# Second attention of a hybrid encoder step: the reciprocal sum applied by a diagonal in the transposing product instead of by a GpSimd pass

## The chip, the cores and the metric

The kernel runs on one core of one Trainium2 chip. The metric is the device time of one execution in microseconds (us); lower is better. A core has five engines with a queue of their own each: TensorE (PE, matrix products; PEld is its weight load), VectorE (DVE), ScalarE (ACT), GpSimd (POOL) and SyncE (SP, which issues the DMAs). They run side by side and wait for each other with semaphores.

## The reference, cut to what matters

Two transformer layers run over 512 prompt tokens and 32 sample tokens. Each layer has two groups of eight attention heads, and the change touches the second group only:

```python
logits = einsum('bqhd,bqkhd->bqhk', qb, ks) * dh ** -0.5
logits = logits + bias
logits = where(valid, logits, -inf)
p = softmax(logits, axis=-1)
return einsum('bqhk,bqkhd->bqhd', p, vs)
```

The kernel does not gather keys. It computes the logits of all keys and adds a large negative number where a key was not among the top-k of its query (the tile `excl`).

## The kernel before, in words

All activations are kept transposed (features on the 128 partitions, 544 tokens along the free dimension). Everything that an engine does is one list of steps (`schedule()`), written out once and walked by each engine's block; an engine does only those steps that concern it, in the order of the list. Two layers are two turns of one loop over this list.

Large products (`G` steps, `L1103` to `L1107`) are made of three products of split operands: `w_hi` is written by ScalarE (`L836`), `w_lo` by GpSimd (`L1623`), from the weights that SP has loaded to `raw`.

The second attention is `b_phase()`. Its unit is a tile: one head and one block of 128 queries, against the keys up to the end of that block, so that tiles are 128, 256, 384 and 512 wide (`b_width`), in chunks of 128 keys. There are 8 heads with 4 blocks each, and two sample tiles of width 288: 34 tiles and 86 chunks in a layer. A tile goes through these steps:

- `BL`: TensorE makes the logits in PSUM (`L1276`, `L1277`). VectorE adds the bias and takes the row maximum (`L1587`) and negates it (`L1589`).
- `BX`: ScalarE takes the exponential into `prob[:, i % 2]` and sums each row into `stat` (`L961`).
- In the `BL` step of the next tile VectorE takes the reciprocal of that sum (`L1593`), and GpSimd multiplies `prob` with it, row by row (`L1638`).
- `BT`, two tiles later: TensorE transposes the chunks of `prob` (`L1286`), and ScalarE copies them to `wts` (`L976`, `L978`, for the sample tiles `L969`, `L970`).
- `BV`, once for each head: TensorE multiplies with the values (`v_product`, `L624`), and VectorE copies the result to `o_t` (`L689`).

The order on TensorE in iteration `i` is `BL(i)`, then `extra[i]`, `BV`, `BT(i - 2)`, and then `late[i]`. The lists `extra` and `late` hold the other work of the phase: the `G` products of the next pair of heads, the sums of their norms (`N`, `L1142`, which wait for ScalarE's squares `L859`), VectorE's norm steps (`E` is `L1475`, `N` is `L1382`, `M` is `L1399` to `L1406`, `W` is `L1417` to `L1430`), the transposes `T` (`L1155`), and on VectorE rounds of top-k of the sample (`TOPK`, `L663`, `L666`). These `G` products end with the fourth pair of heads; the last heads (steps from about 413 us in the first layer) have none beside them until the output projection begins.

## Time and profile before

| | |
|---|---|
| median of 3 runs | 1780.64 us (1780.3 to 1781.72) |
| the profiled execution, its own time | 1778.47 us |
| its span in the trace | 1776.6 us |
| PE busy | 1658.8 us (93%) |
| PEld busy | 1516.1 us (85%) |
| DVE busy | 1014.6 us (57%) |
| ACT busy | 686.6 us (39%) |
| POOL busy | 648.4 us (36%) |
| mean granted TensorE clock | 0.981 of full speed |

Busy shares are averages over stages with different limits. The second attention lies at about 315 to 445 us of the span in the first layer and 1180 to 1306 us in the second. In a row, `xN` is a count; times in brackets are idle time of the engine just before, with what ended it. A plain float32 product stands in the trace with two records of each kind (two PEld, two PE) for each product, a transposing one with one of each.

### The profile page before, as it was taken

Reading aid. Unit: us, or ns where it says so; the run is one execution under the profiler, and the core shown is the slowest. Engines: PE = TensorE matmul, PEld = TensorE weight load, DVE = VectorE, ACT = ScalarE, POOL = GpSimd, SP = SyncE. Lnnn points to the kernel's source line nnn. Section 1 sums busy time; section 2 is a strip of 40 time slices with the busy share of each in tenths; the row PEclk is TensorE's granted clock in tenths of the full one; section 3 lists DMA queues with packets and bytes.
Section 4 is the critical chain, followed back from the end, with each engine's and each line's share of the span. In section 5 each row is a group of like instructions: output and inputs, shape, how many; then the busy total and the mean of one; then the engine's idle time right before and its main releaser. Section 6 shows DMA issues by size and latency. Waiting matters only on the chain.

```text
span 1776.6 us, 33458 instructions
## 1 busy us (share of the span) xinstructions
PE 1658.8 (93%) x11748; PEld 1516.1 (85%) x11762; DVE 1014.6 (57%) x1865; ACT 686.6 (39%) x1282; POOL 648.4 (36%) x352
## 2 busy tenths in 40 slices
PE   6898999887999999999989999989789999999998
PEld 4677888775999999999986878867579999999998
DVE  5466666574566526616656666667636662563366
ACT  3232444344344324424433144534533442342343
POOL 3222332232544334344441232323336434433334
PEclk9899999899899999999999999999989999999999
DMA  5223121210222322322232222121102233233222
GB/s 166 78 64 91 49 55 48 62 43 19 60 84 84 93 86 85 95 84 84 77 88 73 86 68 68 36 76 35 37 25 84 84 93 87 84 90 89 84 82 91
DMA packets 238231, 131.78 MB, mean 74 GB/s; under 512 B 10126, under 2 KB 232062, under 8 KB 238054
## 3 DMA queue, kind: packets, MB, share of 16 engines
q1 hardware_dynamic: 238054, 129.52, 25.5%
q8 instruction: 98, 1.61, 0.4%
q14 instruction: 79, 0.65, 0.1%
HBM read 117.59 MB, written 11.62 MB: 73 GB/s over the span
## 4 chain that ended last, share of the span: by engine, by line
issue 38%; PE 26%; POOL 23%; DVE 7%; ACT 3%; DVEq 1%; ACTq 1%; POOLq 0%; DMA 0%; SPq 0%; another core or an unknown queue 0%
POOL w_lo L1623 20%; PE g_ps L1103 5%; PE g_ps L1104 5%; PE g_ps L1107 5%; PE a_ps L624 2%; POOL h_lo L578 2%; PE a_ps L1181 1%; PE a_ps L1276 1%; PE g_ps L1142 1%; DVE score L1532 1%; POOL sp_lo L1632 1%; PE a_ps L1193 1%; DVE score L666 1%; PE a_ps L1286 1%; ACTq L920 1%
## 5 line engine op out<-in xcount | busy, mean ns | idle before, releaser
L1623 POOL TENSOR_TENSOR w_lo<-raw,w_hi 128x1024 fp32r<-128x1024 f32 (+2 forms) x210 | 503.1, 2396 | 803.2 <-ACT w_hi L836 803.2
L1103 PE MATMUL g_ps<-h_hi,w_hi 128*128 128x272 f32 (+1 forms) x1632 | 452.8, 295 | 17.6 <-DVEq L1492 8.1
L1104 PE MATMUL g_ps<-h_lo,w_hi 128*128 128x272 f32 (+1 forms) x1632 | 444.0, 290 | 0.0
L836 ACT ACTIVATE w_hi<-raw 128x1024 fp32r<-128x1024 f32 (+2 forms) x210 | 217.4, 1035 | 499.1 <-PE g_ps L1107 377.9
L1107 PE MATMUL g_ps<-h_hi,w_lo 128*128 128x272 f32 (+1 forms) x1632 | 340.8, 290 | 0.0
L1103 PEld LDWEIGHTS g_ps<-h_hi,w_hi 128*128 128x128 f32 (+1 forms) x1632 | 309.1, 189 | 29.6 <-issue 18.0
L1104 PEld LDWEIGHTS g_ps<-h_lo,w_hi 128*128 128x128 f32 (+1 forms) x1632 | 308.8, 189 | 0.5
L1107 PEld LDWEIGHTS g_ps<-h_hi,w_lo 128*128 128x128 f32 (+1 forms) x1632 | 257.3, 189 | 0.0
L1501 DVE SCALAR_TENSOR_TENSOR wts<-work,par,wts 128x546 f32<-128x546 f32 x176 | 196.8, 1118 | 100.0 <-ACT wts L1002 92.1
L1103 PE MATMUL a_ps<-h_hi,w_hi 128*128 128x272 f32 x704 | 190.3, 288 | 1.5 <-POOL w_lo L1623 1.5
L1104 PE MATMUL a_ps<-h_lo,w_hi 128*128 128x272 f32 x704 | 190.0, 289 | 0.0
L1107 PE MATMUL a_ps<-h_hi,w_lo 128*128 128x272 f32 x704 | 145.9, 288 | 0.0
L1103 PEld LDWEIGHTS a_ps<-h_hi,w_hi 128*128 128x128 f32 x704 | 132.5, 188 | 1.9 <-POOL w_lo L1623 1.9
L1104 PEld LDWEIGHTS a_ps<-h_lo,w_hi 128*128 128x128 f32 x704 | 132.5, 188 | 0.0
L1107 PEld LDWEIGHTS a_ps<-h_hi,w_lo 128*128 128x128 f32 x704 | 110.1, 188 | 0.0
L1103 PE MATMUL g_ps<-act_hi,w_hi 128*128 128x272 f32 x376 | 102.6, 291 | 4.7 <-DVEq L1514 3.6
L1002 ACT ACTIVATE wts<-work,par 128x546 f32<-128x546 f32 x88 | 74.4, 846 | 75.6 <-DVEq L581 75.5
L1104 PE MATMUL g_ps<-act_lo,w_hi 128*128 128x272 f32 x376 | 101.5, 289 | 0.0
L1638 POOL TENSOR_SCALAR prob<-prob,stat 128x128 f32<-128x128 f32 (+2 forms) x68 | 48.1, 708 | 143.8 <-DVE stat L1593 143.7
L1103 PE MATMUL a_ps<-act_hi,w_hi 128*128 128x272 f32 x328 | 88.8, 289 | 1.2 <-POOL w_lo L1623 1.2
L1478 DVE TENSOR_TENSOR x_t<-x_t,g_ps 128x544 f32<-128x544 f32 x42 | 30.3, 721 | 103.9 <-PE g_ps L1107 102.6
L1104 PE MATMUL a_ps<-act_lo,w_hi 128*128 128x272 f32 x328 | 88.5, 288 | 0.0
(223 smaller groups left out, 2994.1 us busy)
## 6 DMA issues: line engine op xcount, KB each, us to landing
raw<-in_w_up SPq DMA_DIRECT2D x88, 512.0 KB, 3.8
raw<-in_w_in SPq DMA_DIRECT2D x56, 512.0 KB, 3.8
raw<-in_w_down SPq DMA_DIRECT2D x32, 512.0 KB, 3.9
raw<-in_w_out SPq DMA_DIRECT2D x16, 512.0 KB, 3.9
raw<-in_w_down SPq DMA_DIRECT2D x16, 384.0 KB, 3.4
x_nat<-in_x_prompt SPq DMA_DIRECT2D x4, 512.0 KB, 6.4
strip<-bias_line SPq DMA_DIRECT2D x8, 256.0 KB
out_p_av<-v_nat SPq DMA_DIRECT2D x4, 512.0 KB, 3.8
```

The lines of the kernel that those rows point to most:

```text
L578: pool.tensor_tensor(h_lo[:, j, :], prob_f(j), h_hi[:, j, :].bitcast(F32), ALU.subtract).then_inc(x_split.sem, 1)
L624: mm = pe.matmul(a_ps[3][:, c * P:SEQ], v_nat[:, c, p * P:(p + 1) * P], w_view(wts, c), start=(c == 0), stop=(c == QB - 1), skip_group_che ...
L666: dve.match_replace(s, top8[0:n, i, :], s, TAKEN)
L836: act.activation(w_hi[:, n % SPLIT, 0:kt, 0:c], raw[:, n % RAW, 0:kt, 0:c], ACT.Copy).then_inc(hi_done.sem, 1)
L1002: act.activation(cbuf[kind], ubuf[kind][:, 2:U], ACT.Identity, bias=par[:, 3, col:col + 1], scale=par[:, 2, col:col + 1]).then_inc(c_tap.s ...
L1103: pe.matmul(g[0:c, a, 0:HALF], w_hi[:, s, j, 0:c], xh[:, mov], start=(j == 0), stop=False)
L1104: pe.matmul(g[0:c, a, 0:HALF], w_hi[:, s, j, 0:c], xl[:, mov], start=False, stop=False)
L1107: mm = pe.matmul(g[0:c, a, 0:HALF], w_lo[:, s, j, 0:c], xh[:, mov], start=False, stop=(j == kt - 1))
L1478: dve.tensor_tensor(halves(x_t[:, m, :]), halves(x_t[:, m, :]), g, ALU.add)
L1501: dve.scalar_tensor_tensor(c, u[:, tap:tap + U - 2], par[:, tap, col:col + 1], c, ALU.mult, ALU.add)
L1623: pool.tensor_tensor(w_lo[:, s, 0:kt, 0:c], raw[:, n % RAW, 0:kt, 0:c], w_hi[:, s, 0:kt, 0:c].bitcast(F32), ALU.subtract).then_inc(lo_done ...
L1638: pool.tensor_scalar(prob[:, i % 2, 0:w], prob[:, i % 2, 0:w], stat[:, i % 4, 3:4], 1.0, ALU.mult, ALU.mult).then_inc(b_nrm.sem, 1)
```

## The change

GpSimd no longer takes part in the second attention. VectorE, after the reciprocal, waits for its own result (`drain`) and multiplies the 128x128 identity, row by row, with the reciprocal sums; this writes a diagonal matrix into one of two buffers `diag`, which lie over the first 256 columns of `work`. TensorE multiplies each chunk of raw exponentials, as the stationary operand, with that diagonal; the result in PSUM is the transposed and normalised chunk. It waits for `b_diag` where it waited for `b_nrm`. VectorE's wait for `b_nrm` of four tiles before is gone (a semaphore increment stands there).

```diff
+        diag = work[:, 0:2 * P].rearrange("p (a c) -> p a c", a=2)
...
-        b_rcp = ev("b_rcp", btiles)
-        b_nrm = ev("b_nrm", btiles)
+        b_diag = ev("b_diag", btiles)
...
                     elif k == "BT":
                         i = st[1]
-                        pe.wait_ge(b_nrm.sem, b_nrm.at(l, btiles[i]))
+                        pe.wait_ge(b_diag.sem, b_diag.at(l, btiles[i]))
...
                         for c in range((w + P - 1) // P):
                             n = min(P, w - c * P)
-                            mm = pe.transpose(a_ps[2][0:n, c * P:(c + 1) * P], prob[:, i % 2, c * P:c * P + n], ident)
+                            mm = pe.matmul(a_ps[2][0:n, c * P:(c + 1) * P], prob[:, i % 2, c * P:c * P + n], diag[:, i % 2, :], start=True, stop=True)
...
                             dve.wait_ge(bl_full.sem, bl_full.at(l, t))
-
-                            if i >= 4:
-                                dve.wait_ge(b_nrm.sem, b_nrm.at(l, btiles[i - 4]))
-                                dve.sem_inc(spacer, 1)
-                            else:
-                                dve.wait_ge(b_nrm.sem, b_nrm.last(l, btiles[i - 4]))
-                                dve.sem_inc(spacer, 1)
+                            dve.sem_inc(spacer, 1)
+
...
                         if i:
                             dve.wait_ge(b_exp.sem, b_exp.at(l, btiles[i - 1]))
                             s = (i - 1) % 4
-                            dve.reciprocal(stat[:, s, 3:4], stat[:, s, 2:3]).then_inc(b_rcp.sem, 1)
+                            dve.reciprocal(stat[:, s, 3:4], stat[:, s, 2:3])
+                            dve.drain()
+                            dve.tensor_scalar(diag[:, (i - 1) % 2, :], ident, stat[:, s, 3:4], None, ALU.mult).then_inc(b_diag.sem, 1)
...
-                    elif k == "BL" and st[1]:
-                        i = st[1] - 1
-                        w = b_width(btiles[i])
-                        pool.wait_ge(b_rcp.sem, b_rcp.at(l, btiles[i]))
-                        pool.sem_inc(spacer, 1)
-                        pool.tensor_scalar(prob[:, i % 2, 0:w], prob[:, i % 2, 0:w], stat[:, i % 4, 3:4], 1.0, ALU.mult, ALU.mult).then_inc(b_nrm.sem, 1)
```

The order of instructions on SP and ACT is the same in both kernels. On TensorE the place of each instruction stays; what the `BT` steps read changes. This is TensorE's order around the third and fourth tile of a head, of the difference between the two kernels (`cf` holds the identity, `work` the diagonals):

```order
-L1286 MATMUL a_ps<-cf,prob 128x128 x2
+L1286 MATMUL a_ps<-work,prob 128x128 x2
 L1261 REGISTER_ALU
 L1276 MATMUL a_ps<-k_t,q_pad 128x128
 L1277 MATMUL a_ps<-excl,cb 128x128
-L1286 MATMUL a_ps<-cf,prob 128x128 x3
+L1286 MATMUL a_ps<-work,prob 128x128 x3
```

Nothing moved there; each `L1286` product has become a plain one.

On VectorE each tile gets one more instruction. This is the order of the kernel before in the first head, from the maximum of the 512 wide tile to the norm's `W` step (`q_pad`):

```order
L1587 ISA a_ps,stat<-a_ps,strip 128x512
L1587 ISA stat 128x1
L1589 TENSOR_SCALAR stat<-stat 128x1
L1593 RECIPROCAL stat<-stat 128x1
L1417 SCALAR_TENSOR_TENSOR q_pad<-nraw,qk_gain,vb 64x544 x2
```

And this is the same place in the changed kernel (its lines are counted anew):

```order
L1582 ISA a_ps,stat<-a_ps,strip 128x512
L1582 ISA stat 128x1
L1584 TENSOR_SCALAR stat<-stat 128x1
L1588 RECIPROCAL stat<-stat 128x1
L1590 TENSOR_SCALAR work<-cf,stat 128x128
L1417 SCALAR_TENSOR_TENSOR q_pad<-nraw,qk_gain,vb 64x544 x2
```

The diagonal is built behind the reciprocal and ahead of whatever VectorE does next, here the norm's writing of `q_pad`.

## Rows read from the trace of the kernel before

**Rows 1.** Busy time of each engine in both second attentions, with clock
```profile
core 0: us, PE busy (x) PEld busy (x) DVE busy (x) ACT busy (x) POOL busy (x), PEclk, DMA share, GB/s
315.00:445.00 130.00, 108.85 (x623) 83.83 (x628) 77.66 (x228) 55.62 (x150) 38.10 (x40) 0.96 0.15 43
1180.00:1306.00 126.00, 105.03 (x593) 80.29 (x599) 76.70 (x223) 54.89 (x148) 38.12 (x40) 0.96 0.15 44
```

**Rows 2.** Waits of TensorE over the span: who for whom, total, times, longest
```profile
PE a_ps L1286 <- POOL prob L1638: 10.8, 11, 2.0
PE g_ps L1103 <- POOL w_lo L1623: 6.8, 7, 2.3
```

**Rows 3.** Groups by form: busy us, mean ns, then idle time before
```profile
L1286 PE MATMUL a_ps<-cf,prob 128*128 128x128 f32 x168 | 32.4, 293 | 21.4 <-POOL prob L1638 10.8 <-ACT wts L976 9.1 <-ACT wts L970 1.4
L1276 PE MATMUL a_ps<-k_t,q_pad 128*128 128x128 f32 x32 | 6.4, 284 | 0.0
```

**Rows 4.** Timeline of TensorE, first attention: start us, us, engine, line
```profile
290.63 0.38 PE L1201 MATMUL a_ps<-work,cr 128*128 128x128 f32 x2
290.85 0.39 PE L1209 MATMUL a_ps<-work,cr 128*128 128x128 f32 x2
```

**Rows 5.** VectorE's and GpSimd's groups by form
```profile
L1593 DVE RECIPROCAL stat<-stat 128x1 f32<-128x1 f32 x68 | 10.5, 154 | 8.7 <-ACT prob L961 8.2 <-issue 0.5
L1530 DVE TENSOR_SCALAR score<-prob,iw_nat 128x512 f32<-128x512 f32 x2 | 1.0, 487 | 2.3 <-ACT prob L913 2.3
L1530 DVE TENSOR_SCALAR score<-prob,iw_nat 128x256 f32<-128x256 f32 x2 | 0.7, 352 | 3.9 <-ACT prob L913 3.9
L1638 POOL TENSOR_SCALAR prob<-prob,stat 128x256 f32<-128x256 f32 x16 | 12.5, 778 | 49.3 <-DVE stat L1593 49.3
...
L1638 POOL TENSOR_SCALAR prob<-prob,stat 128x128 f32<-128x128 f32 x16 | 9.4, 589 | 16.5 <-DVE stat L1593 16.4
```

**Rows 6.** Timeline, first head of the first layer, all engines
```profile
327.79 0.84 DVE L1401 TENSOR_TENSOR va<-va,vb 128x544 f32<-128x544 f32 x1
328.71 0.72 DVE L1406 SCALAR_TENSOR_TENSOR vb<-va,vb 128x544 f32<-128x544 f32 x1
336.74 0.66 ACT L859 ACTIVATE sq<-nraw 128x544 f32<-128x544 f32 x1 [2.95 <-DVEq L581]
337.54 2.15 PE L1142 MATMUL g_ps<-sq,cf 128*128 128x272 f32 x4 [3.75 <-ACT sq L859]
340.55 1.06 PE L1286 MATMUL a_ps<-cf,prob 128*128 128x128 f32 x4
341.40 1.23 PE L1276 MATMUL a_ps<-k_t,q_pad 128*128 128x384 f32 x2
```

**Rows 7.** Timeline, second pair of heads, all engines
```profile
353.44 1.06 ACT L836 ACTIVATE w_hi<-raw 128x1024 fp32r<-128x1024 f32 x1 [1.51 <-PE g_ps L1107]
355.02 0.63 PE L1286 MATMUL a_ps<-cf,prob 128*128 128x128 f32 x4 [0.75 <-ACT wts L976]
355.92 1.16 PE L1142 MATMUL g_ps<-sq,cf 128*128 128x272 f32 x4 [0.27 <-ACT sq L859]
371.90 0.66 PE L1286 MATMUL a_ps<-cf,prob 128*128 128x128 f32 x4 [0.23 <-POOL prob L1638]
374.01 2.42 PE L624 MATMUL a_ps<-wts,v_nat 128*128 128x512 f32 x8 [0.65 <-ACT wts L978]
```

**Rows 8.** Timeline, third pair and a head without filler, all engines
```profile
409.95 0.63 PE L1155 MATMUL g_ps<-cf,k_t 128*128 128x128 f32 x4 [1.23 <-DVEq L1431]
421.63 0.15 DVE L1593 RECIPROCAL stat<-stat 128x1 f32<-128x1 f32 x1
421.99 1.22 POOL L1638 TENSOR_SCALAR prob<-prob,stat 128x512 f32<-128x512 f32 x1 [0.32 <-DVE stat L1593]
423.26 0.65 PE L1286 MATMUL a_ps<-cf,prob 128*128 128x128 f32 x4 [0.44 <-POOL prob L1638]
```

**Rows 9.** Timeline of TensorE, end of the first layer's phase; last row second layer
```profile
434.91 0.60 PE L1286 MATMUL a_ps<-cf,prob 128*128 128x128 f32 x4
440.52 0.49 PE L1286 MATMUL a_ps<-cf,prob 128*128 128x128 f32 x3
441.72 0.52 PE L1286 MATMUL a_ps<-cf,prob 128*128 128x128 f32 x3 [0.71 <-ACT wts L970]
1275.17 1.06 PE L1286 MATMUL a_ps<-cf,prob 128*128 128x128 f32 x4
```

More of the change, by code:

```diff
@@ L1344, in _ @@
             dve.drain()
-            for s in g_free + [v_done, r_done, e_done, kc_done, i_add, tk_done, a_min, a_sp, s_lo0, o_out, b_max, b_rcp, o_split, sqx_done, c_done, a_prod, a_lo]:
+            for s in g_free + [v_done, r_done, e_done, kc_done, i_add, tk_done, a_min, a_sp, s_lo0, o_out, b_max, b_diag, o_split, sqx_done, c_done, a_prod, a_lo]:
                 dve.sem_inc(s.sem, s.per_layer)
@@ L1608, in _ @@
         def _(pool):
-            for s in (lo_done, s_lo, b_nrm):
+            for s in (lo_done, s_lo):
                 pool.sem_inc(s.sem, s.per_layer)
```

## The prediction, made before the changed kernel ran

> **What bounds the kernel now.** I read the page's busy shares first: TensorE 93%, nothing else above 57% except its own weight load. The change touches only the second attention, so next I read the windows of its two stretches [rows 1]: TensorE is busy 108.9 of 130 us and 105.0 of 126, VectorE 77.7 and 76.7, GpSimd 38 and 38. So TensorE has some 21 us without a matrix product in each stretch, a sixth, and whatever is added to it is paid in full wherever it is not falling into one of these gaps. Third, the waits: over the span TensorE waits 10.8 us in 11 waits for GpSimd's normalised `prob` [rows 2]. That is what the change can remove. Its waits for `w_lo`, the other work of GpSimd, are 6.8 us over the whole span in front of the `g_ps` products [rows 2], and the timeline shows hardly any of them in these stretches, so a freer GpSimd is worth about nothing by itself. Last I walked the timeline of one layer's phase and asked at each `BT` what the next wait of TensorE would be.
>
> **Part 1: the transposing products become plain ones.** There are 86 chunks in a layer, 172 in all. Each is one record now (168 with 128 columns and 4 with 32) [rows 3]. The nearest plain product of the same size, `L1276` with 128 columns, has two records for each product (32 for 16 tiles) of the same length, 284 ns against 293. How far apart they start is told by the first attention: `L1201` and `L1209` are two such products with different weights, and the second starts 0.22 us after the first [rows 4], so 0.11 us a record. So a chunk costs 0.11 us more at the high clock level (2.4 GHz). At the low one (1.2 GHz) four chunks took 0.85 us (340.55 to 341.40, [rows 6]), 0.21 a record, so 0.21 more each. All 172 in the open would be 172 x 0.11 = 18.9 us; none, 0. I take neither end but count the places below.
>
> In these 172 records the weight load could set the pace instead. The products of rows 4 show that it does not at 128 columns, over four records; over eight I have no row, and allow up to 0.15 us a record for the upper end (that is 172 x 0.04 x 2 = 14 us more at worst, all in the open, which I think unlikely).
>
> The Trainium skill ("TensorE: Matmul & The Clock Gate", Terms) says that the transpose mode is 4 times faster for float32, and "Perfetto Trace Analysis" (Transposes) tells one to use it and no plain product. The trace agrees on the direction, not on the size: its rows give a factor of 2 in records and the same length for each. By the factor of 4 each chunk would cost 0.33 us more, and the sum would be up to 57 us. It has 1 chance in 100.
>
> **Part 2: GpSimd's pass becomes VectorE's diagonal.** GpSimd took 0.59 to 0.78 us a tile, and in one place 1.22 us, plus some 0.2 us from the reciprocal's end to its start (421.63 + 0.15 to 421.99) [rows 5, 8]. VectorE now takes the drain, about 0.08 us as between other dependent pairs, and a 128 wide multiply by a column. No row has that width; `L1530` with 512 and 256 takes 487 and 352 ns [rows 5], which is 0.53 ns a column, so 128 would be 0.285 us. Its bounds are the one-column reciprocal, 0.154 us, and the 256 wide one, 0.352. I take 0.285 and with the drain 0.36 us a tile. So the diagonal is ready 0.36 us after the reciprocal, where `prob` was ready after 0.8 to 1.4: 0.5 to 1.0 us sooner. VectorE gets 68 x 0.36 = 24.5 us more, 12 a layer, beside 77.7 of 130: it stays below TensorE, but 0.36 us is paid where VectorE is the one that TensorE waits for.
>
> **The sum, by places, for one layer.**
> - First head. TensorE idles 3.75 us before the `N` products, for a chain of VectorE's norm steps that ends in ScalarE's square (which itself idled 2.95 us for VectorE) [rows 6]. Two diagonals fall in that chain: +0.72. The six chunks before it are hidden by the wait. The four behind it run at the low level: +0.85. One more chunk ahead of `G` products: +0.11. Together 1.7.
> - Second pair of heads (20 chunks). Three chunks lie in front of `G` products and delay them: 0.33. The three at 353 us are hidden: ScalarE's `w_hi`, 1.06 us, holds up what comes next [rows 7]. The four at 355.02 end 0.27 us before the `N` products [rows 7]: 0.44 more is 0.15 in the open. Five at 367 to 369 us are hidden by the wait for the next square. The four at 371.90 start sooner, as they waited for GpSimd, and have until 374.01, where TensorE waits for ScalarE anyway: hidden, but a diagonal ahead of VectorE's `L1382` pushes the norm chain by 0.13. One chunk more at 376: 0.11. Together 0.7.
> - Third pair. The same 0.7, and here TensorE waits 1.23 us for VectorE's `k_t` [rows 8], with a diagonal in the chain: +0.36, and two chunks right behind: +0.22. Together 1.3.
> - The two heads without filler. Here the chain of work runs reciprocal, GpSimd, `BT` [rows 8]. At 421.63 the new diagonal is ready, with the one before it pushing VectorE by 0.36, about 0.5 us sooner than `prob` was; four chunks with 0.44 more eat that up. Net 0 to 0.15 a head, and a chunk behind `BV` 0.11: together 0.4.
> - The end: the wait at 430 us is 0.1 shorter on balance, and then the chunks at 434.91, 440.52 and 441.72 [rows 9] have output products or other waits behind them that move with them: 0.44 + 0.33 + 0.33. Together 1.0.
>
> That is 5.1 us a layer. In the second layer four chunks at 1275.17 are at the low level [rows 9] and so are some at 1285: 0.7 more. 5.1 + 5.8 = 10.9. Against it stands one gain: VectorE's two-input `L1401` takes 0.84 us beside GpSimd's pass and `L1406` 0.72 without it [rows 6]; some 8 such places on the path at 0.1 us give back 0.8. The Trainium skill ("GPSIMD Engine Reference", Key points) says that the two engines share their SBUF interfaces and contend when VectorE reads two inputs from there; by that rule the gain is real, and the trace agrees, with 0.12 us at this place; without the rule the sum would be 10.9.
>
> So +10.1 us. The profiled execution took 1778.47 us (its span 1776.6 and 1.9 around it), which gives 1788.6. The median of the runs is 2.2 above that execution, so the forecast for the median is **1790.7 us**, 0.6% slower.
>
> **The rivals.**
> - *The latency wins* (faster). The 11 waits for GpSimd shrink by 0.5 to 1.0 us each, and the extra records hide, because a `BT` that started sooner still ends before ScalarE wants it. For it: in the heads without filler the chain of work runs through GpSimd. Against it: the point from which it decides is a saving above 0.55 us for a tile of four chunks (5 x 0.11), and only the one 1.22 us pass is clearly above. Its time: 11 x 0.5 = 5.5 less, 1775.1.
> - *The gaps swallow it* (no change). TensorE's 42 us without work are larger than 18.9, and if the extra records fell into them everywhere, the saved waits would pay for the rest: 1780.6, give or take 3. Against it: most gaps are before `N` and `T` steps, and two chunks in five do not stand there.
> - *Everything in the open* (slower still). TensorE pays 18.9 + 1.5 for the low level, and VectorE's diagonals some 2: 1780.6 + 22.4 = 1803. For it: TensorE's share of 84%. Against it: the waits of 0.75 and 3.75 us right beside `BT` steps.
> - *The clock.* TensorE's clock fell to the low level after its 3.75 us of idling. If the changed kernel idles less ahead of the second layer's last heads and keeps the high level there, about 2 us come back; if it falls elsewhere, as much is added. It goes into the range.
> - *The change does not do what it says:* if the plain products had one record each, only part 2 were left, about -3 us: 1777.6. `L1276` speaks against it; it counts with the first rival.
>
> **How the numbers follow.** Forecast 0.70; everything in the open (with the factor of 4) 0.10; no change 0.11; faster 0.09. What a measurement can tell from no change is about 0.2%, 3.6 us; the forecast's own spread (1785 to 1797) is above that. So slower 0.80, same 0.11, faster 0.09. The range goes from 1780, which leaves out the faster rival and some of no change, to 1800.
>
> **What would show it.** In the changed kernel's profile: `L1286` with 336 + 8 records and a gap of 0.11 us between them; the new `TENSOR_SCALAR` with 68 at 0.22 to 0.35 us; no wait of TensorE for `prob`, and new ones for VectorE's diagonal of at most a few us; the stretch of the phase 5 to 6 us longer in each layer, and nothing changed outside. The prediction is wrong if the stretches are not longer, if records start more than 0.13 us apart, or if the diagonal takes over 0.4 us.

## The result, and the profile after

The changed kernel took 1793.78 us (median of 4 runs, 1792.9 to 1796.8), the kernel before 1780.47 us beside it (4 runs, 1774.87 to 1781.72): a ratio of 1.0084, 95% interval 1.0059 to 1.0108 (the ratios here compare all runs of both; the two medians alone give 1.0075). It is slower, by about 13 us where 10 were forecast. Beside the experiments the changed kernel ran again: 1793.55 us against 1776.45, and the ratio was 1.0101 (1.0083 to 1.0118).

The profiled execution took 1793.21 us, its span 1791.3. The two phases of the second attention (from the first logits product `L1276` to the end of the last `L1300`, the sample's product with the values) and the two gated networks behind them, in the changed kernel (start and end, length, busy time and records of TensorE, its weight load, VectorE, ScalarE and GpSimd, granted clock, DMA share, GB/s):

```profile
314.38:450.25 135.87, 120.77 (x716) 96.18 (x722) 88.45 (x260) 55.94 (x150) 14.17 (x6) 0.96 0.14 41
1184.64:1320.49 135.85, 120.74 (x716) 96.19 (x722) 88.44 (x260) 55.93 (x150) 14.16 (x6) 0.96 0.14 41
504.70:886.00 381.30, 373.76 (x2946) 370.96 (x2945) 201.53 (x314) 141.94 (x245) 150.48 (x64) 1.00 0.29 84
1375.00:1755.90 380.90, 373.34 (x2947) 370.53 (x2946) 201.38 (x314) 141.96 (x245) 150.54 (x64) 1.00 0.29 84
```

And the kernel before, between the same marks. The windows of [rows 1] end at other places of the work, so the phases are given again; the rows ahead of the prediction do not show the networks, as nobody looked there:

```profile
315.75:448.34 132.59, 111.44 (x630) 85.94 (x636) 77.22 (x226) 55.62 (x150) 38.10 (x40) 0.95 0.14 42
1178.07:1310.58 132.51, 111.54 (x631) 86.03 (x636) 77.34 (x227) 55.64 (x150) 38.12 (x40) 0.95 0.14 42
503.00:879.70 376.70, 372.41 (x2946) 370.72 (x2945) 194.17 (x314) 142.11 (x245) 151.22 (x64) 1.00 0.30 85
1365.90:1742.60 376.70, 372.43 (x2947) 370.72 (x2946) 194.24 (x314) 142.10 (x245) 151.22 (x64) 1.00 0.30 85
```

In each phase TensorE has 9.3 and 9.2 us more work, VectorE 11.2 and 11.1 more, GpSimd 24 less, and each phase is 3.3 us longer, not the 5 to 6 that the prediction gave as its sign. But the networks, in whose code not one line changed and whose record counts are the same to within one, are some 4 to 5 us longer each. VectorE's busy time is what differs most in them: 7.4 and 7.1 us more for the same 314 records.

Read stage by stage, in us. The attention stage goes from the first logits product to the first norm product (`L1136`) behind the output projection, the network from there to the first product that transposes its tails (`L1161`), which stands close to its end:

| stage | before | after | difference |
|---|---|---|---|
| up to the first attention product of layer 1 | 315.75 | 314.38 | -1.4 |
| attention and output projection, layer 1 | 187.30 | 190.30 | +3.0 |
| network, layer 1 | 376.67 | 381.37 | +4.7 |
| up to the attention product of layer 2 | 298.36 | 298.60 | +0.2 |
| attention and output projection, layer 2 | 187.83 | 190.36 | +2.5 |
| network, layer 2 | 376.65 | 380.86 | +4.2 |
| the rest | 34.09 | 35.49 | +1.4 |

The waits, after (who waits for whom: us in total, times, longest), answering to [rows 2]:

```profile
PE g_ps L1103 <- POOL w_lo L1620: 10.7, 13, 2.3
...
PE a_ps L1103 <- POOL w_lo L1620: 5.4, 8, 0.7
PE a_ps L1286 <- DVE work L1590: 5.1, 7, 1.1
```

The 10.8 us of waiting for `prob` became 5.1 us for the diagonal. The waits for GpSimd's `w_lo`, to which I gave no role, went from 6.8 to 10.7 us and (for `a_ps`) from 2.7 to 5.4.

The new product and the new multiply have the sizes that the forecast gave them. First the two summaries by line (count: minimum, median, maximum in ns), then the products behind the norm sum in the first head:

```profile
L1286 PE MATMUL a_ps<-work,prob x344: 272/275/422, 325.7 to 1313.9; 128*128 128x128 f32 x168, 128*32 128x128 f32 x4
```
```profile
L1590 DVE TENSOR_SCALAR work<-cf,stat x68: 285/286/1445, 320.9 to 1308.0; 128x128 f32<-128x128 f32 x68
```
```profile
335.37 0.66 ACT L859 ACTIVATE sq<-nraw 128x544 f32<-128x544 f32 x1 [3.18 <-DVEq L581]
336.17 1.68 PE L1142 MATMUL g_ps<-sq,cf 128*128 128x272 f32 x4 [3.60 <-ACT sq L859]
...
338.70 1.71 PE L1286 MATMUL a_ps<-work,prob 128*128 128x128 f32 x8
...
340.25 0.81 PE L1276 MATMUL a_ps<-k_t,q_pad 128*128 128x384 f32 x2
```

344 records in place of 172, and 0.285 us for the multiply. Against [rows 6] the eight records at the low level take 1.55 us up to the next product where four took 0.85: +0.70. But the norm sum before them fell from 2.15 to 1.68 and the logits product behind them from 1.23 to 0.81, because less of them ran at the low clock level. Before, the granted clock was at the low level from 335.42 to 342.25 us, over the whole norm sum and most of the logits product; after, from 336.66 to 340.07, so that it fell in the middle of the norm sum and was back ahead of the logits product.

Now the place that nobody had priced. The network works in slices of 128 features, and each slice has an up half and a gate half. For each half VectorE scales TensorE's product into `work` (`L1491`, here called the tap product) and then adds two taps of a short convolution (`L1501`, two records in a row, written as one group with x2); one tap more, ahead of them, is ScalarE's (`L1002`), and ScalarE makes the next `w_hi` right behind it. First and second tap below always mean VectorE's. This is the first part of the network in the kernel before, VectorE's rows and then ScalarE's `w_hi` and GpSimd's `w_lo`:

```profile
533.75 0.85 DVE L1491 TENSOR_TENSOR work<-g_ps,rstd 128x272 f32<-128x272 f32 x3 [0.54 <-issue]
535.64 1.66 DVE L1501 SCALAR_TENSOR_TENSOR wts<-work,par,wts 128x546 f32<-128x546 f32 x2 [1.04 <-ACT wts L1002]
537.49 0.85 DVE L1491 TENSOR_TENSOR work<-g_ps,rstd 128x272 f32<-128x272 f32 x3 [0.19 <-issue]
```
```profile
533.41 2.38 POOL L1623 TENSOR_TENSOR w_lo<-raw,w_hi 128x1024 fp32r<-128x1024 f32 x1 [7.65 <-ACT w_hi L836]
535.51 1.04 ACT L836 ACTIVATE w_hi<-raw 128x1024 fp32r<-128x1024 f32 x1
536.64 2.91 POOL L1623 TENSOR_TENSOR w_lo<-raw,w_hi 128x1024 fp32r<-128x1024 f32 x1 [0.84 <-ACT w_hi L836]
```

And the same instructions in the changed kernel:

```profile
535.04 0.85 DVE L1491 TENSOR_TENSOR work<-g_ps,rstd 128x272 f32<-128x272 f32 x3 [0.19 <-issue]
536.93 4.00 DVE L1501 SCALAR_TENSOR_TENSOR wts<-work,par,wts 128x546 f32<-128x546 f32 x2 [1.04 <-ACT wts L1002]
541.13 0.85 DVE L1491 TENSOR_TENSOR work<-g_ps,rstd 128x272 f32<-128x272 f32 x3 [0.19 <-issue]
```
```profile
535.05 2.39 POOL L1620 TENSOR_TENSOR w_lo<-raw,w_hi 128x1024 fp32r<-128x1024 f32 x1 [7.65 <-ACT w_hi L836]
536.83 1.06 ACT L836 ACTIVATE w_hi<-raw 128x1024 fp32r<-128x1024 f32 x1
537.97 2.38 POOL L1620 TENSOR_TENSOR w_lo<-raw,w_hi 128x1024 fp32r<-128x1024 f32 x1 [0.52 <-ACT w_hi L836]
```

Before, the second tap began at 536.51 us, 0.13 ahead of GpSimd's second pass: it took 0.79 us, and the pass 2.91. After, the pass began at 537.97 and the second tap at 538.11, 0.14 behind it: the tap took 2.83 us, the rest of the pass and 0.59 us more, and the pass 2.38. So the engine that begins second pays. In the fourteen traces of this document 1067 taps begin while a pass has more than 0.2 us to go, and every one of them ends 0.58 to 0.59 us behind that pass. In the changed kernel 7 second taps in each layer are long in this way (at 525, 538, 551, 564, 577, 590 and 603 us), 13.0 us apart; before, one is (at 523), and from 550 us on its slices are 12.0 to 12.2 us apart. They are not free of the contention either: of the four taps of such a slice one takes 1.9 to 2.0 us and one 1.1, where the changed kernel has 2.8 to 2.9 and 1.1. So a long tap costs the network about 1 us, the difference between the two patterns, and not the 2 us that the tap itself loses.

Why does the kernel before win this race at 533 us? The `0.54 <-issue` ahead of the first tap product says it: VectorE stood idle 0.395 us after a register instruction, waiting for nothing, where the same place elsewhere costs 0.19 in all. That delay puts the slice behind GpSimd's first pass and ahead of its second. Counted from the start of the first pass, the first tap begins at 2.23 us instead of 1.88 and takes 0.79 us, where the changed kernel's takes 1.09 beside that pass; so the second tap begins at 3.10 against 3.06, nearly where it was. But ScalarE's `w_hi` is moved with VectorE, and the second pass begins at 3.23 against 2.92. VectorE wins by being late, because what makes GpSimd start is late too.

### The profile page after: what moved, and what is told of

It reads as the page before. It is cut to its first block, busy times and chain, and to the rows that moved or that the text cites. A ratio compares the mean times of both kernels' runs of the same rounds, so it can differ in the third digit from the quotient of the medians.

```text
span 1791.3 us, 33725 instructions
## 1 busy us (share of the span) xinstructions
PE 1676.7 (94%) x11920; PEld 1534.0 (86%) x11934; DVE 1051.4 (59%) x1933; ACT 686.9 (38%) x1282; POOL 598.9 (33%) x284
## 4 chain that ended last, share of the span: by engine, by line
issue 56%; POOL 25%; PE 13%; DVE 4%; ACT 1%; DVEq 0%; POOLq 0%; ACTq 0%; DMA 0%; SPq 0%
POOL w_lo L1620 22%; PE g_ps L1103 3%; PE g_ps L1104 3%; PE g_ps L1107 3%; POOL h_lo L578 1%; PE a_ps L1181 1%; POOL sp_lo L1629 1%; DVE score L1532 1%; DVE sq L570 1%; PE a_ps L1103 1%; PE a_ps L1104 1%; PE a_ps L1107 1%; DVE sq L572 0%; ACT prob L913 0%; PE a_ps L1057 0%
## 5 line engine op out<-in xcount | busy, mean ns | idle before, releaser
L1501 DVE SCALAR_TENSOR_TENSOR wts<-work,par,wts 128x546 f32<-128x546 f32 x176 | 211.2, 1200 | 99.2 <-ACT wts L1002 92.1
L1002 ACT ACTIVATE wts<-work,par 128x546 f32<-128x546 f32 x88 | 74.4, 846 | 119.4 <-DVEq L581 119.2
L1629 POOL TENSOR_TENSOR sp_lo<-work,act_hi 128x384 fp32r<-128x384 f32 (+1 forms) x32 | 35.4, 1127 | 142.3 <-ACT act_hi L930 142.3
```

The source lines that it names most:

```text
L1002: act.activation(cbuf[kind], ubuf[kind][:, 2:U], ACT.Identity, bias=par[:, 3, col:col + 1], scale=par[:, 2, col:col + 1]).then_inc(c_tap.s ...
L1501: dve.scalar_tensor_tensor(c, u[:, tap:tap + U - 2], par[:, tap, col:col + 1], c, ALU.mult, ALU.add)
L1629: pool.tensor_tensor(sp_lo[:, o:o + w], work[:, o:o + w], sp_hi[:, o:o + w].bitcast(F32), ALU.subtract).then_inc(s_lo.sem, 1)
```

## The experiments

They ran in three series, with the kernel before beside them each time: 1776.45 us (median of 13 runs) for 1 to 4, 1776.44 (16) for 5 to 8, and 1776.06 (23) for 9 to 12, the last on another chip than the first two. The ratios compare with the series' own runs. The stages are read from one profiled execution of each kernel. "Long taps" are second records of `L1501` over 2.5 us, in each layer.

**1. The plain products alone.** The kernel before, GpSimd's pass kept, with the products made plain against the identity:

```diff
-  mm = pe.transpose(a_ps[2][0:n, ...], prob[:, i % 2, ...], ident)
+  mm = pe.matmul(a_ps[2][0:n, ...], prob[:, i % 2, ...], ident, start=True, stop=True)
```

> One part of the change alone: the kernel before, with GpSimd's normalising pass kept, and each transposing product of BT made a plain float32 product with the identity. All of the result is computed. Theory (plain products cost 0.11 us a chunk, about a third of it in the open, and the FFN's extra 4.7 us a layer is a collision between VectorE and GpSimd decided by some 10 ns): the second attention becomes 3.5 to 6 us longer in each layer, 7 to 12 us in all, as GpSimd's latency stays; each FFN is either as in the kernel before (0) or 4.2 to 4.7 longer, not in between. So the ratio to the kernel before is 1.004 to 1.006 or 1.009 to 1.012. Rival (the FFN's time comes from what the changed kernel's instructions there are): the FFN is as before, since its instructions are those of the kernel before.

Measured: 1786.93 us, ratio 1.0060 (1.0042 to 1.0079), one long tap. The attention stages were 191.08 and 188.83 us, the networks 376.23 both. The plain products alone cost 10.5 us in the medians, about what the forecast gave for the whole change. Against the expectation the second layer's attention was only 1.0 us longer; but the profiled execution took 1782.90 us, 4.0 below the median of this kernel's runs, so its stages say less than the median does.

**2. The diagonal alone.** The changed kernel with its diagonals built, but not used; TensorE transposes the raw exponentials as before, so that the division by the sums is left out.

```diff
-  mm = pe.matmul(a_ps[2][0:n, ...], prob[:, i % 2, ...], diag[:, i % 2, :], start=True, stop=True)
+  mm = pe.transpose(a_ps[2][0:n, ...], prob[:, i % 2, ...], ident)
```

> The other part alone: the changed kernel with its transposing products kept as they were (with the identity); VectorE still makes the diagonals and TensorE still waits for them, but they are not used, so the normalisation is left out of the result. Theory: GpSimd's latency goes and 172 x 0.11 us of TensorE do not come. The second attention becomes 0 to 3 us shorter in each layer than before (the four waits in the heads without filler shrink by 0.5 us each, the diagonals on VectorE give back 0.4 at two or three places). The FFN is 0 or +4.2 to 4.7 each. Rival (the diagonal on VectorE is what costs in the attention): the attention is 1 to 3 us longer than before in each layer even without the plain products.

Measured: 1781.43 us, ratio 1.0031 (1.0019 to 1.0044). The attention stages were 186.07 and 185.02 us, 1.2 and 2.8 below the kernel before; and yet the kernel was slower, with 7 long taps in each layer and networks of 380.87 and 380.83 us. So GpSimd's pass was worth removing where it stood, and the loss in the networks comes with VectorE's part of the change and not with the products.

**3. The changed kernel again**, for its time beside the others.

> The changed kernel once more, beside the others on the same chip. Theory of the collision: its first FFN part has again seven long taps of 2.8 to 2.95 us, 13.0 us apart, in both layers, and the time is 1.007 to 1.009 of the kernel before. Rival (chance between executions): the pattern is there in one layer or in none, and the time is 1.003 to 1.005.

Measured: 1793.55 us, ratio 1.0101 (1.0083 to 1.0118); 7 long taps in each layer, at the same slices as in the first trace. The ratio is just above the expected 1.007 to 1.009; the pattern is not chance.

**4. A small instruction ahead of the taps.** In seven slices of the changed network VectorE first clears one column of a free tile.

```diff
   dve.wait_ge(g_full.sem, g_full.at(l, ("G", kind, p)))
   g = gview(("G", kind, p))
+  if kind == "ua" and 0 < p < PARTS[0]:
+      dve.memset(top8[:, 0, 0:1], 0.0)
```

> The changed kernel with one one-column memset of some 0.1 us on VectorE ahead of the u-step of each tile 1 to 7 of the first FFN part, a scratch element; all of the result is computed. Theory: VectorE now starts after GpSimd at the tie (GpSimd at 535.05 us, VectorE at 535.04 in the changed kernel), as in the kernel before (533.41 and 533.75), escapes the long taps, and both FFNs give back 4.2 to 4.7 us: the time is 8 to 9.5 us below the changed kernel's, 1.002 to 1.004 of the kernel before. Rival (VectorE's load in the FFN, or something that the attention leaves behind, sets it): seven more instructions on VectorE leave the time as it is or add up to 1 us.

Measured: 1792.49 us, ratio 1.0093 (1.0075 to 1.0110), still 7 long taps. A miss, for the experiment's own reason: the trace has the memset at 535.927 us and the tap product (`L1493` in this kernel) at 535.928. The two overlapped, so VectorE was held up by 0.03 us (0.22 of idle time where 0.19 stood) and not by the 0.1 that was meant; the order was not turned, and the experiment did not test the theory.

**5. GpSimd made to follow.** The changed kernel with one wait more.

```diff
   pool.wait_ge(hi_done.sem, hi_done.at(l, n))
+  if units[n][0] == "ug" and units[n][1] > 0:
+      pool.wait_ge(c_done.sem, c_done.at(l, ("ua", units[n][1] - 1)))
+      pool.sem_inc(spacer, 1)
```

> The changed kernel, with one wait more on GpSimd: in the gated network it makes the w_lo of the gate weights of slice f+1 only when VectorE has finished the two second taps (L1501 of the profile) of the up-projection of slice f. That is all that is changed; nothing is left out. Theory A (the 8.9 us that nothing in the prediction covers come from VectorE's second tap beginning just behind the start of GpSimd's w_lo, and then standing for the rest of that 2.4 us pass; 7 times in each layer where it was once before): with the wait GpSimd always begins behind the taps, no second tap takes over 2 us in the first part of the network, each network takes about 376.5 us again instead of 381.4 and 380.9, and the kernel about 1793.5 - 8.5 = 1785. Rival B (the long taps only show where VectorE had slack, and TensorE's lost time has another cause, as the clock or the weights' DMAs): the taps are short again, the networks stay at 381, and the time stays at 1793. Rival C (the wait itself makes w_lo late: TensorE then waits for g_ps products L1103 on w_lo): the long taps go, but w_lo of the gate arrives up to 1 us late in each slice, and the time is 1793 or more.

Measured: 1783.28 us, ratio 1.0034 (1.0021 to 1.0048), no long tap, networks of 375.97 and 375.34 us. A wait more makes the changed kernel 10.3 us faster. The long taps are the cause of what the networks lost.

**6. One delay of VectorE.** The changed kernel; once in each layer, at the third slice, VectorE copies 128 columns and drains.

```diff
+  if (kind, p) == ("ua", 2):
+      dve.tensor_copy(prob[:, 0, 0:P], ident)
+      dve.drain()
```

> The changed kernel, with VectorE held up once in each layer: ahead of the first tap (L1491) of the third slice of the up-projection it copies the 128x128 identity over a free buffer and drains, about 0.36 us, at the place where it stood idle for 0.395 us longer in the kernel before (533.36 to 533.75 us in its first layer). Nothing else is changed. Theory A (which of the two engines begins first is handed on from slice to slice, and one delay of 0.4 us decides it for the layer's part): 0 to 2 long second taps in place of 7 in each layer, networks at 376 to 377 us, kernel about 1785. Rival B (the order is set anew in every slice by when ScalarE's w_hi comes, whatever happened before): one slice changes, at least 5 long taps stay, kernel 1792 to 1794. Rival C (the 0.4 us of idle time was a consequence and not the cause, and VectorE's place in its stream of instructions does it): as B in the time, with the copy seen in the trace and the pattern unchanged.

Measured: 1784.45 us, ratio 1.0036 (1.0023 to 1.0049); one long tap in each layer, networks of 376.74 and 376.26 us. VectorE's timeline at that slice:

```profile
536.37 0.23 DVE L1438 COPY prob<-cf 128x128 f32<-128x128 f32 x1 [0.19 <-issue]
536.68 0.85 DVE L1494 TENSOR_TENSOR work<-g_ps,rstd 128x272 f32<-128x272 f32 x3
538.58 1.72 DVE L1504 SCALAR_TENSOR_TENSOR wts<-work,par,wts 128x546 f32<-128x546 f32 x2 [1.04 <-ACT wts L1002]
```

The tap product begins 0.31 us after the copy, both taps together take 1.72 us where they took 4.00, and all later slices stay in the good order. So each slice inherits the order of the one before: 0.3 us once is worth 4.6 us.

**7. The kernel before, with VectorE's stream moved by 24.** The increments are on a semaphore that nobody waits for.

```diff
+  if (kind, p) == ("wo", 3):
+      for _ in range(24):
+          dve.sem_inc(spacer, 1)
```

> The kernel before, with 24 semaphore increments on VectorE (on a semaphore that nobody waits for) behind the last step of the output projection, far from any wait of the network; they move VectorE's later instructions along in its stream and take less than 1 us in a place where VectorE has slack. Nothing else is changed. Theory A (the 0.395 us in which VectorE issues nothing ahead of the first tap at 533.36 us stands at a fixed place of its instruction stream, and the change moved it by adding 34 drains and taking out 32 waits in the loop over layers): the gap lies at another instruction, 5 to 7 long second taps come in each layer, the networks take about 381 us, and the kernel 1776.5 + 8.5 = 1785. Rival B (the gap belongs to that instruction, by what came before it in time): gap and pattern stay, 1 long tap in each layer, time 1776 to 1777. Rival C (the gap moves, but another one comes early enough to do the same): 1 to 3 long taps, time 1776 to 1779, with the gap seen elsewhere.

Measured: 1775.50 us, ratio 0.9995 (0.9985 to 1.0004). The time missed what theory A expected and was nearest to rival C's; the gap moved, as both said. Its trace has no pause ahead of the third slice's tap product (the idle time there is 0.19 again). It has one of 0.43 us between 521.13 and 521.56, behind the first 1343 of VectorE's records, where it also stands in the kernel before. That now falls on the signal behind the second slice's tap product, one slice earlier, so the taps behind it begin late:

```profile
520.25 0.85 DVE L1494 TENSOR_TENSOR work<-a_ps,rstd 128x272 f32<-128x272 f32 x3 [0.19 <-issue]
522.49 1.66 DVE L1504 SCALAR_TENSOR_TENSOR wts<-work,par,wts 128x546 f32<-128x546 f32 x2 [1.39 <-ACT wts L1002]
```

1.39 us of idle time stands there instead of 1.04. The good order begins one slice sooner, no tap is long, and the networks take 375.18 us, the shortest of any. A shift can turn the order either way.

**8. VectorE normalises the exponentials themselves**, and TensorE transposes.

```diff
-  dve.tensor_scalar(diag[:, (i - 1) % 2, :], ident, stat[:, s, 3:4], None, ALU.mult)
+  pw = b_width(btiles[i - 1])
+  dve.tensor_scalar(prob[:, (i - 1) % 2, 0:pw], prob[:, (i - 1) % 2, 0:pw], stat[:, s, 3:4], None, ALU.mult)
```

> The changed kernel, but VectorE multiplies the exponentials themselves with the reciprocal sums (128 to 512 wide, in place, instead of the identity 128 wide), and TensorE transposes them as in the kernel before. GpSimd stays out of the second attention. Nothing is left out. The experiment with the diagonals built and not used gave 1781.43 us with seven long second taps in each layer, and attentions of 186.1 and 185.0 us. Theory A (TensorE's plain products are the whole price of the change inside the attention; VectorE has room): the pass on VectorE takes about 0.28 us at 128 wide and about 0.4 to 0.5 at 512, 0.1 to 0.2 more than the diagonal; attentions of 185.5 to 187.5 us, below the 190.3 of the changed kernel, long taps as there, kernel about 1782 (1780 to 1785). Rival B (VectorE's chain is as dear as TensorE's products: each maximum of the next tile waits for the pass): attentions of 188 to 190 us and 1786 to 1790.

Measured: 1783.49 us, ratio 1.0039 (1.0026 to 1.0053), 7 long taps; the multiply's median is 0.420 us, the attention stages 186.37 and 188.96 us. It is 10.1 us faster than the diagonal.

**9. The changed kernel, with VectorE's stream moved by 62**, spread over the output projection.

```diff
+  if kind == "wo":
+      for _ in range(8 if p < 6 else 7):
+          dve.sem_inc(spacer, 1)
```

> The changed kernel, with 62 semaphore increments more on VectorE in each layer (on a semaphore that nobody waits for), 8 or 7 ahead of each wait of the output projection, where VectorE stands idle for 1.4 us in every tile; an increment takes 0.09 us there, so they fit. Nothing else is changed. In the experiment with 24 increments the idle 0.4 us stood at the same count of VectorE's records as in the kernel before (number 1343), which is then another instruction. In the traces of both kernels such gaps come at numbers 128 apart (1343, 1471, 1727, 1855). Theory A (the gap belongs to a position in VectorE's stream of instructions, every 128 records, and what follows from it decides the order of the engines in the network): 62 more records put number 1471 on the first tap (L1491) of the third slice, where the kernel before has its gap; 0 to 2 long second taps in each layer in place of 7, networks at 376 to 377 us, kernel 1793.5 - 9 = 1784.5. Rival B (the order in the network follows from something else that the change did, as the time at which the network begins): 7 long taps stay and the time stays at 1792 to 1794.

Measured: 1792.14 us, ratio 1.0090 (1.0075 to 1.0105), 7 long taps. A miss. VectorE's records grew by 55 in each layer and not by 62 (seven increments left no record), and number 1471 fell on the drain behind the first tap, at 536.35 us, where the tap itself, already running, covers it. The tap product had no pause:

```profile
534.45 0.85 DVE L1494 TENSOR_TENSOR work<-g_ps,rstd 128x272 f32<-128x272 f32 x3 [0.19 <-issue]
536.34 3.97 DVE L1504 SCALAR_TENSOR_TENSOR wts<-work,par,wts 128x546 f32<-128x546 f32 x2 [1.04 <-ACT wts L1002]
```

So it neither supports theory A nor speaks against it: the gap was not brought where it was wanted.

**10. The kernel before, with its stream moved by 66.** As number 9, with 8 and 9 in place of 8 and 7.

> The mirror of the experiment with 62 increments: the kernel before with 66 semaphore increments more on VectorE in each layer, 8 or 9 ahead of each wait of the output projection. Nothing else is changed. They put number 1343 on the norm's L1400, where the changed kernel has it and where VectorE waits anyway, and number 1471 on a tap L1501 seven slices on. Theory A (position in the stream decides): the 0.4 us of idle time at the third slice goes, 5 to 7 long second taps come in each layer, networks at 380 to 381.5 us, kernel 1776.5 + 8.5 = 1785. Rival B (the pattern belongs to the kernel before as such): 1 long tap in each layer, 1776 to 1777.

Measured: 1785.98 us, ratio 1.0056 (1.0041 to 1.0072), 7 long taps in each layer, networks of 381.71 and 381.16 us. That is what theory A expected. Its timeline around the third slice:

```profile
532.28 0.85 DVE L1494 TENSOR_TENSOR work<-g_ps,rstd 128x272 f32<-128x272 f32 x3 [0.19 <-issue]
534.17 4.09 DVE L1504 SCALAR_TENSOR_TENSOR wts<-work,par,wts 128x546 f32<-128x546 f32 x2 [1.04 <-ACT wts L1002]
538.45 0.85 DVE L1494 TENSOR_TENSOR work<-g_ps,rstd 128x272 f32<-128x272 f32 x3 [0.19 <-issue]
```
```profile
532.29 2.38 POOL L1626 TENSOR_TENSOR w_lo<-raw,w_hi 128x1024 fp32r<-128x1024 f32 x1 [7.66 <-ACT w_hi L836]
535.28 2.39 POOL L1626 TENSOR_TENSOR w_lo<-raw,w_hi 128x1024 fp32r<-128x1024 f32 x1 [0.61 <-ACT w_hi L836]
```

This is the picture of the changed kernel, row for row, in a kernel whose attention is the old one. Here too the shift came out 7 short (59 records), so number 1343 fell on an instruction at 508.32 us, a little behind the one that I had meant, but as meant away from the third slice. Instructions that do nothing cost the kernel before 9.9 us.

**11. Experiments 8 and 5 together.**

> Two earlier edits together: VectorE multiplies the exponentials with the reciprocal sums and TensorE transposes them (1783.49 us with seven long taps in each layer), and GpSimd makes the gate's w_lo only behind VectorE's second tap of the slice before (which took 10.3 us from the changed kernel). Nothing is left out. Theory A (the two are independent): no long taps, networks at 375.3 to 376, attentions at 186 to 189, kernel about 1783.5 - 10.3 = 1773.2, some 3 us below the kernel before. Rival B (the gain of the wait is in part a gain that the kernel before has already, and the attention on VectorE costs 1 to 2 us): 1775 to 1778.

Measured: 1775.13 us, ratio 0.9998 (0.9989 to 1.0007), no long tap. It is 8.2 us faster than number 5, but not measurably faster than the kernel before: the time is the one of rival B (1775 to 1778), not of theory A (1773.2). This was the candidate for a version that beats both; it only draws level.

**12. The kernel before with the wait of experiment 5.**

> The kernel before with the same wait on GpSimd alone: the gate's w_lo behind VectorE's second tap of the slice before. Nothing is left out. Theory A (the wait takes away only what the long taps cost; the kernel before has one in each layer, about 1.0 to 1.5 us a layer in TensorE's time): networks at 375.3 to 376 us, kernel 1776.4 - 1.5 = about 1775. Rival B (the wait is worth 10 us whatever the kernel): 1766.

Measured: 1774.69 us, ratio 0.9992 (0.9982 to 1.0002). The interval holds no change; the networks are 375.34 and 375.96 us, 1.0 us shorter on the mean of the two. One tap of 2.7 us is left in each layer, at 656 and 1517 us, where the second part of the network begins. The wait is worth little where the order was good already.

The thirteen kernels (medians in us, from all three series) fall into four cells:

| | good order (0 or 1 long tap) | 7 long taps in each layer |
|---|---|---|
| transposing products | 1776.06 (before), 1775.50 (7), 1775.13 (11), 1774.69 (12) | 1781.43 (2), 1783.49 (8), 1785.98 (10) |
| plain products | 1786.93 (1), 1783.28 (5), 1784.45 (6) | 1793.55 (3), 1792.49 (4), 1792.14 (9) |

The means are 1775.3 and 1783.6 above, 1784.9 and 1792.7 below. The products cost 9.5 us in the one column and 9.1 in the other; the long taps 8.3 in the one row and 7.8 in the other. The two add up, and each is about half of the loss of 17 us. The change goes from the top left cell to the bottom right one. The cells hold kernels that differ in more than the products, so the single pairs scatter: where the products alone differ they cost 10.5 us (the kernel before and 1) and 12.1 (2 and 3), and where the transposing kernel of the pair has VectorE normalise the exponentials, 8.2 (11 and 5) and 10.1 (8 and 3).

## Why the prediction was right, and where it was not

- **The number** was 1790.7 us, the median 1793.78, inside the range. That it came so close is in part luck: two errors stood against each other. Between the two profiled executions, 14.7 us apart, the attention stages cost 5.5 us where the sum had 10.1, and three places outside them, on which the forecast had said "nothing changed outside", cost 10.3. That is the statement that failed. The sign for the phase, 5 to 6 us longer in each layer, failed too: it was 3.3.
- **Two records for each product, 0.11 us a record: right.** 344 records, and TensorE's work grew by 9.3 us a layer, as 86 times 0.11 gives. In the comparison of the two traces a tile of four chunks holds up what follows by 0.40 to 0.47 us at the high level, of three by 0.34 to 0.39, of two by 0.23, of one by 0.11 to 0.12.
- **The weight load as the pace, and the factor of 4: did not come.** Eight records in a row, on the changed kernel's timeline, take 1.13 us; without the 0.28 of the last that is 0.12 from start to start:

```profile
413.97 1.13 PE L1286 MATMUL a_ps<-work,prob 128*128 128x128 f32 x8
```

- **The diagonal at 0.285 us: right** (median 0.286). Its upper bound, 0.352 us, was no bound: eight of the 68 passed it, six with 1.34 to 1.45 us and two with 0.83, all beside GpSimd's `w_lo`.
- **The gain of 0.8 us from `L1401`: the records bear it out.** Six of them took 0.84 us before, and none more than 0.73 after, 0.7 us in all; how much of it lay on the path was not measured.
- **First head, 1.7 forecast, 0.5 measured** (from 320 us on; in the first 5 us of the phase the changed kernel had gained 0.35, where the low level ended sooner). The norm chain grew by 0.35 and not by 0.72. The four chunks at the low level cost 0.70 (forecast 0.85), but the norm sum and the logits product gave back 0.47 and 0.42, as less of them ran at the low level. The rival on the clock had the mechanism, though it named the second layer only; the sum had left it out.
- **Second pair, 0.7 forecast, 1.0 measured; third pair, 1.3 and 0.4.** The delay of VectorE's `k_t` by a diagonal did not come: TensorE's wait of 1.23 us for it [rows 8] shrank to 0.92, and the product at 412.9 us, which had waited for `prob`, began 0.6 us sooner. **Two heads without filler, 0.4 and 0.2. The end, 1.0 and 1.3.** In all that is 3.4 us against 5.1; with the gain ahead of 320 us and the sample's products at the end the first layer's phase cost 3.3, its stage with the output projection 3.0. The second layer's phase cost 3.3 against 5.8, its stage 2.5. The low clock level that I had charged 0.7 for, and had expected to keep, did not come: before, the granted clock was low for 3.4 us from 1274.08 and again from 1284.32; in the changed kernel it was not low between 1211 and 1316 us.
- **Over all traces** the size is firmer than over these two. The seven kernels with plain products have attention stages of 190.80 and 190.33 us in the mean (189.5 to 192.3 and 188.8 to 191.7), the seven with transposing ones 186.94 and 187.29 (186.1 to 188.0 and 185.0 to 189.4): 3.9 and 3.0, together 6.9 us where 10.1 were forecast. Single traces of kernels with the same attention differ by 1 to 4 us there.
- **The latency wins (the faster rival): half true.** With the diagonal alone (2) the attention is 4.0 us shorter over both layers than in the kernel before, and 3.6 shorter than the mean of the four traces with the old attention, though one of these four comes within 1.5 us of it; and 2 is 4.6 us faster than 10, which has the old attention and the same order in the networks. But with their double records the products cost 12.1 us more (3 against 2): they do not hide.
- **The networks, 0 forecast, 8.9 measured.** The forecast said that a freer GpSimd was worth nothing and asked nothing about what else VectorE's new instructions shift. They add 66 records to VectorE's stream ahead of the network (the norm's `L1400` is number 1343 where it was 1277) and with that move the pause that had put the engines into the good order. That the long taps cost it is shown (5, 6 and 10), and that the place in the stream decides it is borne out by 10 (no pause at the third slice, and the bad order) and by 7 (the pause at the same number, one slice earlier, and the good order); 9 did not test it.
- **The last writes, 0 forecast, 1.4 measured.** SyncE's last wait, for the outputs to land, takes 3.1 to 3.8 us in the seven traces with plain products and 1.8 to 2.2 in the seven others, without an exception. The landing of the last output, in the kernel before and in the changed one (KB and median us from issue to landing):

```profile
out_y_s<-xs_nat SPq DMA_DIRECT2D x1, 128.0 KB, 2.3
```
```profile
out_y_s<-xs_nat SPq DMA_DIRECT2D x1, 128.0 KB, 3.7
```

TensorE has been done for 2 us by then, and the same bytes are written. Why stays open; no run was made for it.

Put together: 6.9 in the attention and some 1.6 in the last writes is 8.5, against 8.6 us between experiments 5 and 12, which differ in the change alone and are both in the good order. The other 8 are the order in the networks.

## What to carry to other kernels

Doubling the records of a small product costs its full 0.11 us wherever no wait stands behind it. Of the 18.9 us that 172 products make, 10.5 to 12.1 showed in the time (1, and 3 against 2), with TensorE busy for 84% of the phase before the change; the cheaper step on another engine (here 0.36 us in place of 0.8 to 1.4) gave back about 4. When a stage whose code did not change gets slower, compare its instructions one by one in both traces and look for those that are longer, before looking for a cause in the change: here 14 instructions of 2.8 to 2.9 us stood where half of the result came from. And where two engines start long passes within 0.2 us of each other, the order between them is better fixed by a wait than left to whatever precedes it; it cost nothing here, and it may keep the next edit's time readable.

## What the runs showed of the hardware

- **The engine that starts second stands.** A VectorE pass with two inputs (128x546, 0.79 us alone) that begins 0.14 us behind the start of GpSimd's two-input pass (128x1024, 2.38 us alone) takes 2.83 us, until 0.59 us after that pass ends; over all long taps of the changed kernel it is 2.82 to 2.95. If it begins 0.13 us ahead, it takes 0.79 and GpSimd's pass 2.91. The Trainium skill ("GPSIMD Engine Reference", Key points) says that VectorE instructions with two inputs in SBUF contend with GpSimd; the traces agree, and show that it is not a slowing by 0.12 us, as the forecast took it from `L1401`, but a stand for the whole remaining pass. That `L1401` (327.79 us) fits it too: it began 0.51 us behind GpSimd's 0.79 us pass and ended 0.57 behind its end, as the taps do. The diagonal, which reads one tile, also stands beside `w_lo`; its eight slow records end 0.08 us behind the pass.
- **A pause at places 128 records apart.** VectorE issues nothing for 0.38 to 0.45 us in some places although it waits for nothing. In the first layer of each trace these stand behind record numbers that lie a multiple of 128 apart (1215, 1343, 1471 and 1727 before, 1855 after, 1343, 1855 and 1983 in experiment 7), at whichever instruction falls there; behind a running instruction or inside a wait they are not seen. In the second layer they stand at the same instructions of the loop, though the loop's 1956 records are no multiple of 128 (the one at the tap product again, at 1396.62 us in the kernel before). So the place belongs to the program and not to a running count. The page of the changed kernel lists a queue for instructions,

```profile
q14 instruction: 75, 0.61, 0.1%
```

0.61 MB in 75 packets, 8.1 KB each. Such a packet of 8,192 bytes begins 0.67 us after the end of the pause at 533.75 us in the kernel before, and 0.71 after that of experiment 7. That a pause is the step to another block of 128 instructions is my reading, not shown; the packet comes behind the pause and does not cover it.
- **An increment of a semaphore is not free, nor always visible:** they start 0.09 us apart where several follow each other on VectorE (7), and with 62 written VectorE's records grew by 55 (9).
- **A one-column memset hardly delays what follows it** where that does not depend on it: in experiment 4 it takes 59 ns, the next instruction begins 1 ns behind its start, and the two together begin 0.03 us later than the one did.
